# Masks on GpSimd, a loop on TensorE and a turned copy on VectorE in the inverse of an RWKV-7 chunk, with a reordered preparation

## Reference

```python
def step(state, inp):
    r_t, w_t, k_t, v_t, a_t, b_t = inp
    sa = jnp.einsum('bhvk,bhk->bhv', state, a_t)
    state = (state * w_t[:, :, None, :] + sa[..., None] * b_t[:, :, None, :]
             + v_t[..., None] * k_t[:, :, None, :])
    return state, jnp.einsum('bhvk,bhk->bhv', state, r_t)
...
bonus = jnp.sum(rh * kh * r_k.astype(jnp.float32), axis=-1, keepdims=True) * vh
return (y + bonus.reshape(B, S, W)) * g
```

## Time and profile before

| what | value |
|---|---|
| median of 3 runs | 1270.4 us (1269.38 to 1272.56) |
| profiled execution, its own time | 1270.97 us |
| span of that execution | 1269.2 us |
| PE, DVE, ACT, POOL busy | 1229.3, 682.6, 552.0, 527.7 us |
| slabs 26 to 29 and preparation | 194.3 to 223.3 us in the span |
| entry to the inverse | 223.3 to 252.7 us |
| the four full rounds and the last `next_x` | 252.7 to 288.9 us |

### The profile page before, as it was taken

One profiled execution on the slowest core, in us unless ns is written; L12 is line 12 of the kernel. 1 busy time (PEld: TensorE's weight loads), 2 busy tenths in 40 slices (PEclk: granted clock), 3 DMA queues, 4 the chain that ended last, 5 costly groups with the idle time before them and its releaser, 6 DMA issues.

```text
span 1269.2 us, 20861 instructions
## 1 busy us (share of the span) xinstructions
PE 1229.3 (97%) x8361; PEld 993.7 (78%) x8361; DVE 682.6 (54%) x821; ACT 552.0 (43%) x749; POOL 527.7 (42%) x245
## 2 busy tenths in 40 slices
PE   9999999887999999999999999999999999999997
PEld 6887777777878777888888888888777777777876
DVE  8877558776595432453142141344488765442832
ACT  5344562434534333532132232235243478885242
POOL 4333336403576422654444444446443322333453
PEclk9999999999999999999999999999999999999998
DMA  7552122100362211322222222322422421112221
GB/s 270 188 160 84 67 67 67 53 4 5 107 226 100 82 52 34 113 87 100 100 95 90 97 100 100 100 95 91 155 83 83 125 67 53 65 67 67 100 100 67
DMA packets 35099, 119.40 MB, mean 94 GB/s; under 512 B 4544, under 2 KB 4800, under 8 KB 34624
## 3 DMA queue, kind: packets, MB, share of 16 engines
q1 hardware_dynamic: 30624, 106.19, 24.7%
q10 hardware_dynamic: 4384, 11.93, 2.9%
HBM read 110.50 MB, written 2.10 MB: 89 GB/s over the span
## 4 chain that ended last, share of the span: by engine, by line
PE 75%; DVE 17%; ACT 3%; issue 3%; DMA 0%; DVEq 0%; POOL 0%; POOLq 0%; SPq 0%; ACTq 0%
PE banks L1446 20%; PE banks L1448 20%; PE banks L1447 20%; DVE y_mid L868 2%; DVE qk L868 1%; PE banks L1940 1%; PE banks L1956 1%; PE banks L2045 1%; PE banks L2030 1%; DVE qk_lo L868 1%; DVE x_res L876 1%; PE banks L1691 1%; DVE vv L868 1%; DVE yk L868 1%; DVE a_lo L868 1%
## 5 line engine op out<-in xcount | busy, mean ns | idle before, releaser
L386 POOL TENSOR_TENSOR w_lo<-w_raw,w_hi 128x1024 fp32r<-128x1024 f32 x144 | 352.3, 2448 | 509.9 <-ACT w_hi L442 509.7
L442 ACT ACTIVATE w_hi<-w_raw 128x1024 fp32r<-128x1024 f32 x144 | 152.7, 1061 | 307.1 <-PE banks L1448 205.7
L1448 PE MATMUL banks<-a_hi,w_lo 128*128 128x512 f32 x608 | 237.1, 390 | 0.0
L1446 PE MATMUL banks<-a_hi,w_hi 128*128 128x512 f32 x576 | 229.0, 398 | 3.8 <-DVE a_lo L868 1.7
L1447 PE MATMUL banks<-a_lo,w_hi 128*128 128x512 f32 x576 | 224.4, 390 | 0.0
L1448 PE MATMUL banks<-b_hi,w_lo 128*128 128x512 f32 x384 | 149.5, 389 | 0.0
L868 DVE TENSOR_TENSOR x_res<-banks,x_res 128x512 f32<-128x512 f32 x62 | 42.9, 692 | 180.7 <-PE banks L1448 178.1
L1446 PEld LDWEIGHTS banks<-a_hi,w_hi 128*128 128x128 f32 x576 | 108.2, 188 | 34.1 <-issue 8.1
L1448 PEld LDWEIGHTS banks<-a_hi,w_lo 128*128 128x128 f32 x608 | 114.1, 188 | 24.4
L386 POOL TENSOR_TENSOR w_lo<-w_raw,w_hi_mlp 128x1024 fp32r<-128x1024 f32 x36 | 87.2, 2423 | 109.5 <-ACT w_hi_mlp L442 109.5
L1447 PEld LDWEIGHTS banks<-a_lo,w_hi 128*128 128x128 f32 x576 | 108.2, 188 | 21.5 <-issue 0.2
(11 more groups left out here) (392 smaller groups left out, 2326.4 us busy)
## 6 DMA issues: line engine op xcount, KB each, us to landing
w_raw<-in_weights SPq DMA_DIRECT2D x188, 512.0 KB, 3.2
x_in<-in_x SPq DMA_DIRECT2D x4, 512.0 KB, 7.7
decay<-in_decay ACTq DMA_DIRECT2D x1, 2048.0 KB, 7.7
rot<-raw SPq DMA_DIRECT2D x32, 64.0 KB, 2.6
x_res<-in_x ACTq DMA_DIRECT2D x4, 512.0 KB, 3.8
consts<-in_consts SPq DMA_DIRECT2D x1, 1093.0 KB, 11.1
q_twice<-q_twice ACTq DMA_DIRECT2D x8, 128.0 KB, 2.9
k_stack<-qk_lo ACTq DMA_DIRECT2D x8, 128.0 KB, 2.6
```

The costliest lines, as they stand in the source:

```text
L386: nc.gpsimd.tensor_tensor(o, a, b, op).then_inc(S(name), 1)
L442: return nc.scalar.activation(o, a, f, **kw)
L1446: mm(o, high[:, w], hi[:, kc, :], start=kc == first, stop=False)
L1448: done = mm(o, w_lo[:, s % 4, w], hi[:, kc, :], start=False, stop=kc == last)
```

## The change

1. GpSimd gets 20 new multiplications, five levels times four tiles: `NL[:, f]` = N * mask of the level, before `next_x` of that level. The mask is turned (`<` for `>`), and `next_x` uses `NL` in place of N, so its result needs no mask. The names `x0_ready` and the new `level_ready` are one count.
2. VectorE's four masked copies of a level become plain copies: tiles 0 and 2 on VectorE, tiles 1 and 3 on ScalarE. The `XT` copy of tile 3 moves from ScalarE to VectorE (`turned_last`), ahead of `memory_lo`.
3. TensorE's four rounds are a loop over a register; its waits compare with values computed from the register, and each of them also increments `level_step`, for which nothing waits.
4. The bonus factor moves to the head of a tile's iteration on VectorE (`bonus_factor`), ahead of `bonus(f - 1)`; `pt` has two buffers; TensorE's `bonus` also waits for the normalised `kk`, which frees its bank. GpSimd takes `kx` and `rx` first and `ax` last, after `a_ready`.
5. `ret_gate(0)` and `chunk_decays` move behind the first `take_abr` pieces. Some semaphores are merged (`chunk_done`, `heads_normed`).

```diff
@@ GpSimd
-                    mul(ax[:, f, :], ax[:, f, :], e_neg[:, f, :], "decayed")
                     mul(kx[:, f, :], kx[:, f, :], e_neg[:, f, :], "decayed")
                     mul(in_chunks(rx[:, f, :]), in_chunks(rx[:, f, :]), e_cum[:, f, :, 1:CH + 1], "decayed")
+                    pool.wait_ge(S("a_ready"), f + 1)
+                    mul(ax[:, f, :], ax[:, f, :], e_neg[:, f, :], "decayed")
...
+                    pool.wait_ge(S("tok_done"), 2 * TT)
+                    for lv in range(5):
+                        mask = C("mask_level", lv * CH, CH).unsqueeze(1).broadcast_to([P, TT, CH])
+                        mask = mask.unsqueeze(1).broadcast_to([P, 2, TT, CH])
+                        for f in range(NF):
+                            if lv == 0:
+                                pool.wait_ge(S("abr_ready"), f + 1)
+                                pool.wait_ge(S("akr_done"), f + 1)
+                            else:
+                                pool.wait_ge(S("nx_done"), NF * (lv - 1) + f + 1)
+                            mul(NL[:, f], ABR[:, f, :, :, 0, :], mask, "level_ready")
@@ ScalarE
-            for f in range(NF):
-                turned(f)
-            for lv in range(4):
-                for f in range(NF):
-                    turned(NF * (lv + 1) + f)
-                memory_hi(2 * lv)
-                memory_hi(2 * lv + 1)
+            for lv in range(5):
+                for f in range(3):
+                    turned(NF * lv + f)
+                for f in (1, 3):
+                    act.wait_ge(S("nx_done"), NF * lv + f + 1)
+                    actv(turned_slots(ak_tile(f, 0)), chunks(pair(f)), copy).then_inc(A("xt_px_ready"), 1)
+                if lv < 4:
+                    memory_hi(2 * lv)
+                    memory_hi(2 * lv + 1)
@@ VectorE
+            def bonus_factor(f):
+
+                if f >= 2:
+                    dve.wait_ge(S("bonus_done"), f - 1)
+                stt(pt[:, f % 2, :], rx[:, f, :], V("r_k", f), kx[:, f, :], ALU.mult, ALU.mult).then_inc(D("rk_ready"), 1)
...
                 if s >= S_RG - 1:
                     f = s - S_RG + 1
+                    if f < NF:
+                        bonus_factor(f)
                     if f >= 1:
                         bonus(f - 1)
...
-            ret_gate(0)
-            chunk_decays()
             take_abr(0)
             take_abr(1)
+            chunk_decays()
...
+            ret_gate(0)
             ret_gate(1)
...
+            def turned_last(lv):
+
+                dve.wait_ge(S("xt_done"), NF * (lv + 1))
+                cp(XT[:, 3].rearrange("p h t c -> p (h t c)"), psum[6][:]).then_inc(D("px_xt_ready"), 1)
+
+            turned_last(0)
             for lv in range(5):
-                for f in range(NF):
+                for f in (0, 2):
                     dve.wait_ge(S("nx_done"), NF * lv + f + 1)
-                    tt(turned_slots(ak_tile(f, 0)), chunks(pair(f)), mask, ALU.mult).then_inc(D("px_ready"), 1)
+                    cp(turned_slots(ak_tile(f, 0)), chunks(pair(f))).then_inc(D("px_xt_ready"), 1)
...
+                if lv < 4:
+                    turned_last(lv + 1)
                 if 1 <= lv < 4:
                     memory_lo(2 * lv - 2)
                     memory_lo(2 * lv - 1)
@@ TensorE
             for f in range(NF):
-                pe.wait_ge(S("xt_ready"), f + 1)
+                if f < 3:
+                    pe.wait_ge(S("xt_px_ready"), f + 1)
+                else:
+                    pe.wait_ge(S("px_xt_ready"), 1)
+                pe.wait_ge(S("level_ready"), NF + f + 1)
                 next_x(f)
-            for lv in range(4):
+            with pe.Fori(1, 5) as r:
                 for f in range(NF):
-                    pe.wait_ge(S("px_ready"), NF * lv + f + 1)
-                    pe.wait_ge(S("xt_ready"), NF * lv + f + 1)
+                    if f % 2 == 0:
+                        pe.wait_ge(S("px_xt_ready"), r * 3 + (f // 2 - 1)).then_inc(S("level_step"), 1)
+                    else:
+                        pe.wait_ge(S("xt_px_ready"), r * 5 + (f // 2 - 1)).then_inc(S("level_step"), 1)
                     x_px(f)
                 for f in range(NF):
-                    pe.wait_ge(S("xn_ready"), NF * lv + f + 1)
+                    pe.wait_ge(S("xn_ready"), r * NF + (f + 1 - NF)).then_inc(S("level_step"), 1)
                     turn(f, 2 * f)
                 for f in range(NF):
-                    pe.wait_ge(S("xt_ready"), NF * (lv + 1) + f + 1)
+                    if f < 3:
+                        pe.wait_ge(S("xt_px_ready"), r * 5 + (f + 1)).then_inc(S("level_step"), 1)
+                    else:
+                        pe.wait_ge(S("px_xt_ready"), r * 3 + 1).then_inc(S("level_step"), 1)
+                    pe.wait_ge(S("level_ready"), r * NF + (NF + f + 1)).then_inc(S("level_step"), 1)
                     next_x(f)
```

More of the change, by code:

```diff
@@ L193, in hybrid_blocks @@
         XT = at("XT", 142, [P, NF, 2, TT, CH])
+        NL = at("NL", 152, [P, NF, 2, TT, CH])
         AT = at("AT", 126, [P, NF, 2, TT, HD])
@@ L402, in _ @@
                         pool.wait_ge(S("n_ready"), f + 1)
-                        mul(x0, x0, ident8, "x0_ready", ALU.add)
+                        mul(x0, x0, ident8, "level_ready", ALU.add)
+                    pool.wait_ge(S("tok_done"), 2 * TT)
[9 more added lines that the diff above has]
+                            mul(NL[:, f], ABR[:, f, :, :, 0, :], mask, "level_ready")
                     for f in range(NF):
@@ L606, in turned @@
                 act.wait_ge(S("xt_done"), n + 1)
-                actv(XT[:, f].rearrange("p h t c -> p (h t c)"), psum[2 * f][:], copy).then_inc(A("xt_ready"), 1)
+                actv(XT[:, f].rearrange("p h t c -> p (h t c)"), psum[2 * f][:], copy).then_inc(A("xt_px_ready"), 1)
             tok(0)
@@ L1122, in memory_lo @@
                     ALU.mult, ALU.subtract).then_inc(D("mem_lo_ready"), 1)
+            def turned_last(lv):
+                dve.wait_ge(S("xt_done"), NF * (lv + 1))
+                cp(XT[:, 3].rearrange("p h t c -> p (h t c)"), psum[6][:]).then_inc(D("px_xt_ready"), 1)
+            turned_last(0)
             for lv in range(5):
-                mask = C("mask_level", lv * CH, CH).unsqueeze(1).broadcast_to([P, TT, CH])
-                mask = mask.unsqueeze(1).broadcast_to([P, 2, TT, CH])
-                for f in range(NF):
+                for f in (0, 2):
                     dve.wait_ge(S("nx_done"), NF * lv + f + 1)
-                    tt(turned_slots(ak_tile(f, 0)), chunks(pair(f)), mask, ALU.mult).then_inc(D("px_ready"), 1)
+                    cp(turned_slots(ak_tile(f, 0)), chunks(pair(f))).then_inc(D("px_xt_ready"), 1)
                 for f in range(NF):
@@ L1146, in _ @@
             for f in range(NF):
-                dve.wait_ge(S("bc_done"), f + 1)
+                dve.wait_ge(S("chunk_done"), f + 1)
                 scale = sc[:, f, :].rearrange("p (t u) -> p u t", u=2).unsqueeze(3).broadcast_to([P, 2, TT, HD])
@@ L1151, in _ @@
             for f in range(NF):
-                dve.wait_ge(S("at_done"), f + 1)
+                dve.wait_ge(S("chunk_done"), NF + f + 1)
                 tt(AT[:, f], chunks(whole(f))[:, :, 1:2 * TT:2, :], ident_add, ALU.add).then_inc(D("at_ready"), 1)
@@ L1557, in bonus @@
                 pe.wait_ge(S("rk_ready"), f + 1)
-                mm(psum[6 + f % 2][:], C("blockones"), pt[:, 1, :], start=True, stop=True).then_inc(S("bonus_done"), 1)
+                pe.wait_ge(S("heads_normed"), NF + f + 1)
+                mm(psum[6 + f % 2][:], C("blockones"), pt[:, f % 2, :], start=True, stop=True).then_inc(S("bonus_done"), 1)
             pe.wait_ge(S("dve_step"), 2)
@@ L1712, in next_x @@
                                 r, t = slice(CH * p, CH * p + CH), 2 * tp + u
-                                last = mm(place(2 * f + p, u, 2 * h + tp), ABR[r, f, h, t, 0, :], X[r, f, h, t, :], start=True, stop=True)
+                                last = mm(place(2 * f + p, u, 2 * h + tp), NL[r, f, h, t, :], X[r, f, h, t, :], start=True, stop=True)
                 last.then_inc(S("nx_done"), 1)
@@ L1759, in chunk_states @@
                             last = mm(place(2 * f + p, h, t), k_tok[r, t, e:e + HD], v_tok[r, t, e:e + HD], start=False, stop=True)
-                last.then_inc(S("bc_done"), 1)
+                last.then_inc(S("chunk_done"), 1)
             def transitions(f):
@@ L1769, in transitions @@
                             last = mm(o, GH[r, 2 * f + h, t, 0, :], ABR[r, f, h, t, 1:3, :], start=True, stop=True)
-                last.then_inc(S("at_done"), 1)
+                last.then_inc(S("chunk_done"), 1)
             def y_inputs(f):
@@ L1834, in _ @@
             for f in range(NF):
-                pe.wait_ge(S("x0_ready"), f + 1)
+                pe.wait_ge(S("level_ready"), f + 1)
                 if f < 2:
@@ L1907, in _ @@
                         spread_parts(psum[4 + f][:], f, hrn_both[:]).then_inc(S("gn_spread_done"), 1)
```

(6 more changed lines are left out.)

8 lines of the change are left out of this document (3 added, 5 removed).

## The result

The changed kernel takes 1274.25 us in the median of 20 runs (1271.5 to 1276.78), the kernel before 1270.11 (1268.08 to 1274.36, 20 runs on the same chip): ratio 1.0027, 95% interval 1.0021 to 1.0033. It became slower by 0.27%, where 0.17% faster was forecast. The profiled execution took 1274.55 us around a span of 1272.8, so 3.58 more than the one before; the medians differ by 4.1 and the ratio says 3.4.

What follows compares the result with a forecast made beforehand. VectorE was taken to bound the preparation and instruction fetching TensorE's rounds. Entry -2.4 and rounds +0.25 gave -2.15 us, from 1270.97 to 1268.8 us; range 1263 to 1281.

Steps and rivals of the forecast that it cites:

- the price of the loop's new code: TensorE's first pass through the loop: about 592 new instructions, fetched at 253 per 3.6 us, would take 8.4 us.
- the entry: Preparation up to the first `next_x`: earlier `pt` and gates bring it 2.4 us earlier, bounds -1.2 and -3.2.
- `mem_lo`: VectorE's two pieces in passes 3 and 4: one GpSimd mask comes between, making rounds 8.4 us, against 7.35 without collision.
- the clock: TensorE in the rounds: assumed not to fall in the sum; where it does, a `turn` costs 1.6 us more.
- passes 1 and 2: TensorE's first two rounds: 8.4 us for fetching new code, then 7.4 with code held, 6.2 of work plus 1.2 of waits.
- passes 3 and 4: TensorE's last two rounds: 8.4 us each, with one GpSimd piece colliding with `mem_lo`.
- to `last_xt`: Way from the last pass to `last_xt`: 3.85 us with the collision, against 2.66 before.
- the rest, behind `last_xt`: Everything else, such as merged semaphores and `level_step`: no instruction added in a tight place, 0 us.
- the register waits: TensorE's 16 waits per round on register values: 0.075 us each, 1.2 per round, bounds 0 and 2.4.
- The code that is held: TensorE's loop: later passes take their code from what TensorE still holds, without fetching; the forecast's case, chance 0.42.
- the rival that fetches again: TensorE's loop: passes 2 to 4 fetch their code again, 11.5 us each, total 1279.1 us; chance 0.26.
- collisions and waits at their dear end: Rival: two GpSimd pieces between each `mem_lo`, 0.15 us per wait, one fallen `turn`, entry gain 1.2: 1275.2 us; chance 0.10.

Runs made afterwards that it cites:

- experiment 2: The changed kernel with VectorE's two `mem_lo` pieces ahead of `turned_last` instead of behind it: 1269.57 us, ratio 0.9992 to the kernel before.
- experiment 7: The changed kernel with `mem_lo` ahead of `turned_last` and the 1 MB memory load issued later, behind ScalarE's GH copies: 1268.26 us, ratio 0.9977 to the kernel before.
- experiment 1: The changed kernel with TensorE's four rounds written out and their waits on constants: 1273.89 us, ratio 1.0021 to the kernel before.
- experiment 5: The changed kernel with `mem_lo` ahead of `turned_last` and TensorE's rounds written out with constant waits: 1271.92 us, ratio 1.0011 to the kernel before.
- experiment 4: The kernel before with only the preparation's part of the change (parts 4 and 5): 1270.57 us, ratio 1.0001 to the kernel before.
- experiment 6: Experiment 4's kernel with GpSimd also computing the 20 masked matrices, which nobody reads: 1269.88 us, ratio 0.9993 to the kernel before.
- experiment 8: Experiment 4's kernel with the 1 MB memory load issued later, behind ScalarE's GH copies: 1267.69 us, ratio 0.9978 to the kernel before.
- experiment 10: The kernel before with only the 1 MB memory load issued later, behind ScalarE's GH copies: 1270.22 us, ratio 0.9999 to the kernel before.
- experiment 11: Experiment 8's kernel with TensorE's loop; masked copies stay on VectorE, no masks on GpSimd: 1266.67 us, ratio 0.9974 to the kernel before.
- experiment 3: The changed kernel with the 1 MB memory load issued later, behind ScalarE's four GH copies: 1272.94 us, ratio 1.0022 to the kernel before.
- experiment 9: The changed kernel with the preparation's part (parts 4 and 5) undone: 1276.49 us, ratio 1.0047 to the kernel before.

## Why the prediction was wrong

**The step that failed is the price of the loop's new code**, 592 instructions at 3.6 us for 253, and behind it stand the entry, `mem_lo` and the clock. The forecast of the profiled execution was 1268.8 us, it took 1274.55: 5.7 more. By the terms of the sum:

| term | forecast | measured | difference |
|---|---|---|---|
| passes 1 and 2 | 8.4 + 7.4 | 11.77 + 7.63 | +3.60 |
| passes 3 and 4 | 2 x 8.4 | 2 x 9.23 | +1.66 |
| to `last_xt` | 3.85 | 2.83 | -1.02 |
| entry | -2.4 | -1.25 | +1.15 |
| the rest, behind `last_xt` | 0 | 0.34 | +0.34 |

- *The new code, passes 1 and 2.* The forecast let the packets come 3.6 us apart and end with the first pass. In the changed kernel they moved at 252.0, 257.25 and 262.75 us, the third within the second pass. 1.5 of the 3.6 us are a fallen `turn` (3.48 for 1.97). The rest comes back in other traces: experiments 2 and 7, at a clock of 1.00, take 17.95 and 18.02 us for the two passes, 2.2 over the forecast's 15.8, with packets 4.25 to 5.5 us apart. It is not the loop as such: written out, with the same copies (experiments 1 and 5), these two passes take 18.04 and 18.03. That pass 2 alone came near its forecast (7.63 for 7.4) was luck: the first had been so long that the third packet was there; with a shorter first pass it takes 8.55 and 8.81. Why the packets come later than 3.6 us is open.
- *`mem_lo`.* The mechanism, the place and the three prices were right: 7.35, 8.4 or 9.2 us for none, one or two GpSimd pieces. I took one, because the register waits should let `mem_lo` start first. The trace shows GpSimd 0.12 us ahead, so each of the two pieces waits for a mask: 9.23 twice. Experiment 2 confirms it, 4.4 us. That sum also charged `last_xt` 3.85 us, where 2.83 was measured: no mask is left for GpSimd behind the fifth, so the third `mem_lo` pair is free. I missed that, and it hid 1.0 us of the error. So the forecast had charged 3.15 us for the collision already (1.05 three times), and in the sum this term is off by 0.64 alone. It decides the sign all the same: without the collision the kernel is no slower than before (experiment 2).
- *The clock*, which I had left out of the sum ("where it does, a `turn` costs 1.6 more"). In the profiled execution it falls after the stall of 2.57 us (0.79 in the 8 us from 232), and again after the stalls of the first pass, to the 1.2 GHz level for a `turn` (granted clock 0.50 from 261 to 263 us). It need not: in the traces of experiments 1, 2, 4, 5 and 6 it stays at 1.00 behind stalls of 2.0 to 2.7 us at the same place. Over many executions the holes do show. The mean granted clock was 0.9964 to 0.9967 in the kernels with neither the stall of the entry nor the collision (before, experiments 7, 8, 10 and 11), 0.9952 to 0.9959 with the stall alone (2, 4, 5 and 6), 0.9929 and 0.9936 with the collision alone (3 and 9), and 0.9939 and 0.9946 with both (the changed kernel and 1). Among executions of one and the same kernel 0.001 of clock goes with 0.64 us (212 executions; uncertainty 0.12), so the 0.0027 between the changed kernel and the one before goes with an estimated 1.7 us. This is a correlation: no run holds the clock fixed. The changed kernel's quickest execution, 1271.5 us, is one at 0.997.
- *The entry.* `k_tok` came at 245.99 (246.0 forecast), and that is partly luck: the products were 0.8 earlier than forecast (2.8 for 2.0), and the stall and the clock behind it took this and more. The gates collided, as in the forecast's bound of -1.2 (three took 4.38 us), but `k_tok` waited only 0.21 for them. Wrong was the step that nothing else moves with the preparation. The earlier preparation starts the 1 MB load on ScalarE's queue 2.8 us earlier, and the packet of instructions due next, whose predecessor TensorE entered near 227 us, is moved only near 231, at the end of the load; in experiments 3, 7, 8 and 11, with the load later, it is moved between 228.0 and 229.25. I had costed the instructions that move and not this DMA. In the profiled execution the fallen clock behind the stall took 1.23 us more, as much as the 1.15 that the entry lacks. Over many executions experiments 4, 8 and 10 settle the load as a table of two by two: nothing for the preparation alone (+0.0001), nothing for the later load alone (-0.0001), and -0.0022 together.
- *The code that is held* was right, and the rival that fetches again was wrong: no packet moved between 263 and 292 us, and no "issue" stall stands in passes 2 to 4 (the 0.27 us in pass 2 is told of above). The Trainium skill (Runtime: NRT & Kernel Launch, section Instruction fetch mechanics) says both that TensorE's instruction store holds 2048 instructions and that a taken branch outside the current two-page window forces a fetch; by the first a body of some 590 stays inside, which the trace bears out, by the second passes 2 to 4 would have been near 11.5 us (the prediction's estimate), which they are not. The branch goes back over more than two packets of instructions.
- *The register waits.* Two per tile ahead of `next_x` make that phase 2.54 us in place of 2.10: 0.055 for each of eight waits. With constants in the same waits it is 2.09 (experiment 1, passes 3 and 4). One per tile shows nothing: `x_px` stays at 2.10 here, and so does `next_x` in experiment 11. Ahead of `turn` at most 0.16 stands before the fourth, and that is put down to VectorE. A pass without other trouble takes 7.1, so 0.9 over the 6.2 of its matmuls; 1.2 had been taken.

The rival *collisions and waits at their dear end* was given 0.10 and 1275.2 us. Three of its four terms happened: two GpSimd pieces between the `mem_lo`, a fallen `turn`, an entry of -1.25. Its wait of 0.15 us and its 4.65 for `last_xt` were too dear, the first pass, 8.4 there too, too cheap, and the small entry came of the stall and the clock, not of the gates. So its 1275.2 lies near the measured time partly by luck.

**Left open.** In the versions with the split copies and the rounds written out (experiments 1 and 5) packets come 3.5 to 5.0 us apart, 4.2 on average, where VectorE's masked copies, written out too, give 3.6 to 3.8 on average (experiments 4, 6 and 8). The loop's three packets come 4.0 to 5.5 us apart with either kind of copies (experiment 11: 4.75 and 5.0). GpSimd's masks are not the cause (experiment 6), register waits are not (there are none in these versions). What is, no run tells.

## What to carry to other kernels

A piece with two SBUF inputs on VectorE and one on GpSimd that come due at the same time in a loop can collide in every pass, as here in both passes that had the two; look for the stretch in which GpSimd waits, and put it there (4.4 us here for moving two pieces). When work is moved ahead, list each DMA that starts with it and what else is on the 16 DMA engines then: a large load can hold back the next packet of instructions, and the gain with it. A loop pays only where fetching is the last of the bounds; see first what the next one is, here VectorE at the same 7.7 us. Price its first pass by itself: it was the forecast's largest error. And compare a mended change with the part of it that costs nothing: here the preparation and the later load alone were as fast as the whole (experiments 7 and 8).

## What the runs showed of the hardware

- A TensorE loop of some 590 instructions runs its later passes with no instruction packet at all (none from 263 to 292 us), and the whole kernel moves 60 packets in place of 66. In experiment 11 one packet moves in these passes, at 270.75 us.
- A packet of TensorE's instructions that meets a 1 MB load on all 16 DMA engines is late: TensorE stands for 2.0 to 2.7 us in six kernels with the load at 226.2 to 227.2 us (2.57 changed kernel, 2.60, 2.02, 2.32, 2.74 and 2.29 experiments 1, 2, 4, 5 and 6), and for 0.27 us or not at all in four with the same preparation and the load after 237 us (7; 3, 8 and 11). The transfers in the 8 us from 226, DMA share in tenths and GB/s in 40 slices:

```profile
DMA  0000009902709879899798702000000000000000
GB/s 0 0 0 0 0 0 287 123 0 82 205 41 492 369 328 532 369 410 492 328 492 369 328 0 82 0 0 0 0 0 0 0 0 0 0 0 0 0 0 0
...
q10 hardware_dynamic: 144, 1.05, 38.5%
q8 instruction: 1, 0.02, 0.7%
```

- Waits on a value computed from a register cost TensorE 0.44 us for eight of them, two per tile, where small matmuls follow each other without a gap (2.54, against 2.09 with constants in experiment 1), and nothing visible where there is one per tile (2.10).
- The new code of a loop of some 590 instructions is dearer than its packets at 3.6 us: 17.95 and 18.02 us for the first two passes at a clock of 1.00 (experiments 2 and 7), 15.8 by that price.
